# A two-layer hybrid attention decoder: the layer norm's statistics reordered on VectorE and TensorE, and spread by transposes

## The chip, the cores and the metric

The program runs on one core of one Trainium2 chip. The metric is the device time of one execution in microseconds; several executions are timed, and their median is given. One more execution is recorded by the hardware profiler, and all durations below come from that one.

## What is computed

Two decoder layers over 512 tokens of 1024 channels, in float32. Each layer has a mixing sub-layer and a feed-forward sub-layer, and each of them ends in a layer norm, so the program holds four layer norms in a row of dependent steps:

```python
u = x * (1.0 + sc1) + sh1
mix = token_mixer(u, w_in[l], ...)
x = layer_norm(ALPHA * x + (1.0 + g1) * mix, ln1_g[l], ln1_b[l])
u = x * (1.0 + sc2) + sh2
x = layer_norm(ALPHA * x + (1.0 + g2) * swiglu(u, w_ffn_in[l], w_ffn_out[l]), ln2_g[l], ln2_b[l])

def layer_norm(x, g, b):
    mu = jnp.mean(x32, -1, keepdims=True)
    var = jnp.mean(jnp.square(x32 - mu), -1, keepdims=True)
    return ((x32 - mu) * lax.rsqrt(var + EPS) * g + b).astype(x.dtype)
```

## The kernel before

Activations lie with channels on the 128 partitions: a tile of 1024 channels by 512 tokens is eight chunks (KD = 8) of 128x512. The residual stream is the tile `res`. A weight matrix is used in blocks of 128 output channels, called jobs: SyncE loads a block into one of two slots of `ring`, ScalarE rounds it into `w_hi` (L633), VectorE takes the rest into `w_lo` (L895, `prepare`; `prepare_behind` says with which chunk it is done), and TensorE multiplies three times for each pair of 128 channels: high by high (L1463), high by low input (L1464), low by high (L1465). The input of each sub-layer is split the same way into `u_hi` and `u_lo`. Every engine's instruction stream is written out by hand, in the order of the program text, and semaphores tie the streams together.

The layer norm after the mixing uses the chunks `wo0` to `wo7`, the one after the feed-forward the chunks `fo0` to `fo7`. For chunk m VectorE, in `layernorm`, does the split of a later weight block, subtracts a common shift from `res` (`unshift`, L1002; the shift is a channel sum that TensorE left in the bank `shift_ps`), adds the gated result of the sub-layer (L1017), adds the chunk to the running sum `t2` (L1035) and the squared chunk to the running sum of squares in `squares[:, 0]` (`add_square`, L1007). ScalarE makes the squares (L697). `link` makes the engine wait until the instruction it wraps has finished. The last chunk, m = 7, is not added to the running sums.

After the last chunk TensorE, in `mean_and_variance` (L1659 on), works in this order:

- `columns(mean_col, t2)`: four matmuls with one column each, which sum the seven chunks in `t2` over the partitions for 4x128 tokens (L1670); then the same for `res[:, 7]`, once L1017 has written it. This gives the mean, one token per partition, four columns.
- `columns(var_col, ...)`: the same for `squares[:, 0]` and `squares[:, 7]`.
- `keep_busy(2)`: two matmuls of 128x512 whose result nobody reads (L1685).
- `spread(mean_ps, 0)`: four matmuls of a broadcast column of `ln_s` with the identity, which put the mean of each token on all partitions (L1677). It waits for VectorE's copy of the mean (L1051).
- `keep_busy(4)`, then `spread(rstd_ps, 3)` for the reciprocal standard deviation, which waits for VectorE's reciprocal (L1057), then `keep_busy(9)` except in the last norm.

VectorE meanwhile does the weight split that the next sub-layer begins with, then `ada_part1` or `ada_part2` (`fold`, L978 to L983: five operations on 128x8 and a memset, which fold the norm's weights into the next input's scale and bias; only norms 0, 1 and 2 have it), then the four statistics operations: copy of the mean (L1051), its square (L1053), variance (L1055), and after ScalarE's square root (L702) the reciprocal (L1057). Then, chunk by chunk, it subtracts the spread mean (L1062) and multiplies by the spread reciprocal (L1065). ScalarE makes the new input from that (L644, L645), VectorE its low part (L1072), and TensorE's `project_first` starts on three weight blocks at once, chunk by chunk, as the chunks come. After the last norm TensorE turns `res` back to tokens on partitions (L1802) and the result is stored.

Numbering in this text: norm 0 and norm 1 are those of layer 0 (after mixing, after feed-forward), norm 2 and norm 3 those of layer 1.

Of the kernel before, what the change touches and what calls it, by code (L numbers as in the profile page):

```python
# [9 lines left out]
D_MODEL, SEQ, DEPTH = 1024, 512, 2  # L10
# [13 lines left out]
P = 128  # L24
# [173 lines left out]
def build(nc, x, w_ada, b_ada, c, w_in, pe_k, w1_k, w2_k, pe_v, w1_v, w2_v, lam, norm_g,  # L198
# [5 lines left out]
    with ctx:  # L204
# [50 lines left out]
        squares = at("squares", 46, KD)  # L255
# [56 lines left out]
        cos, sin, ident = cst[:, C_COS:C_COS + SEQ], cst[:, C_SIN:C_SIN + SEQ], cst[:, C_ID:C_ID + P]  # L312
# [3 lines left out]
        ln_s = sb("ln_s", [P, 4, TT])  # L316
# [23 lines left out]
        shift_ps, mean_col, var_col = banks[:, 2, :], banks[:, 3, 0:TT], banks[:, 4, 0:TT]  # L340
# [71 lines left out]
        sq_summed = sem("sq_summed")  # L412
# [27 lines left out]
        def wait_saved(eng, l, name):  # L440

            if name in THIRD:
                eng.wait_ge(third_saved, len(THIRD) * l + THIRD.index(name) + 1)
                return
            n = chunk(l, name)
            eng.wait_ge(chunk_saved[n % 2], n // 2 + 1)
# [431 lines left out]
        def _(dve):  # L878
# [3 lines left out]
            def link(ins):  # L882


                count[0] += 1
                ins.then_inc(dve_chain, 1)
                dve.wait_ge(dve_chain, count[0])
# [9 lines left out]
            def prepare_behind(l, name):  # L897
                for job in prepared_at(l, name):
                    prepare(*job)
# [6 lines left out]
            for k in FIRST_DVE:  # L906
# [3 lines left out]
                else:  # L910
                    ins = V.scalar_tensor_tensor(first_sum, ada_first[k], c_silu[:, k:k + 1], first_sum,
                                                 ALU.mult, ALU.add)
# [55 lines left out]
            def ada_part1(l):  # L968

                fold(l - 1, V_LN2G, V_LN2B, ada[:, l, 8:16], ada[:, l, 0:8], 0, 1, part1)  # L970

            def ada_part2(l):
                fold(l, V_LN1G, V_LN1B, ada[:, l, 32:40], ada[:, l, 24:32], 1, 0, part2)
# [22 lines left out]
            def layernorm(l, which):  # L996
                n = 2 * l + which
                names = [f"wo{m}" if which == 0 else f"fo{m}" for m in range(KD)]
                last_norm = l == DEPTH - 1 and which == 1
                def unshift(m):  # L1000

                    return V.scalar_tensor_tensor(res[:, m, :], shift_ps, -float(KD), res[:, m, :], ALU.mult, ALU.add)  # L1002

                def add_square(m):

                    dve.wait_ge(squared, n * KD + m + 1)
                    return V.tensor_tensor(squares[:, 0, :], squares[:, 0, :], squares[:, m, :], ALU.add)  # L1007

                for m in range(KD):
                    prepare_behind(l, names[m])  # L1010
                    if n >= 1 and m == 0:

                        dve.wait_ge(res_ready, n * KD)
                    if m >= 2:
                        link(unshift(m))
                    wait_done(dve, l, names[m])
                    V.scalar_tensor_tensor(res[:, m, :], bank_of(l, names[m]), gate1[:, l, which, m:m + 1],  # L1017
                                           res[:, m, :], ALU.mult, ALU.add).then_inc(saved(l, names[m]), 1)
                    if n == 0 and m == 4:
                        save_ada(2)  # L1020
                    elif n == 1 and m < 6:
                        add_ada_ffn(2 * KF + 2 * m)
                        add_ada_ffn(2 * KF + 2 * m + 1)
                        if m in (1, 4):
                            save_ada(7 + m // 4)
                    if m == 1:
                        dve.wait_ge(shift_done, n + 1)
                        wait_saved(dve, l, names[1])
                        for k in range(2):
                            unshift(k).then_inc(shifted, 1)  # L1030
                        dve.wait_ge(shifted, 2 * n + 2)
                        link(V.tensor_tensor(t2, res[:, 0, :], res[:, 1, :], ALU.add))
                    elif 2 <= m < KD - 1:
                        wait_saved(dve, l, names[m])
                        ins = V.tensor_tensor(t2, t2, res[:, m, :], ALU.add)  # L1035
                        if m == KD - 2:
                            ins.then_inc(y_summed, 1)
                        else:
                            link(ins)
                        link(add_square(m - 1))  # L1040
                        if m == KD - 2:
                            add_square(m).then_inc(sq_summed, 1)
                if not last_norm:
                    prepare(l + which, FIRST_SPLIT[which])
                if which == 0:
                    ada_part2(l)
                elif l + 1 < DEPTH:
                    ada_part1(l + 1)
                mean_s, var_s, rstd_s, square_s = (ln_s[:, k, :] for k in (0, 2, 3, 1))
                dve.wait_ge(mean_done, n + 1)  # L1050
                V.tensor_copy(mean_s, mean_col).then_inc(mean_saved, 1)  # L1051
                dve.wait_ge(mean_saved, n + 1)
                link(V.tensor_tensor(square_s, mean_s, mean_s, ALU.mult))  # L1053
                dve.wait_ge(var_done, n + 1)
                V.tensor_tensor(var_s, var_col, square_s, ALU.subtract).then_inc(var_ready, 1)  # L1055
                dve.wait_ge(std_ready, n + 1)
                V.reciprocal(rstd_s, var_s).then_inc(rstd_saved, 1)  # L1057
                for m in range(KD + 1):
                    if m < KD:
                        if m == 0:  # L1060
                            dve.wait_ge(mean_spread, n + 1)
                        link(V.tensor_tensor(res[:, m, :], res[:, m, :], mean_ps, ALU.subtract))  # L1062
                        if m == 0:
                            dve.wait_ge(rstd_spread, n + 1)
                        V.tensor_tensor(res[:, m, :], res[:, m, :], rstd_ps, ALU.mult).then_inc(normed, 1)  # L1065
                    if m and not last_norm:
                        sub_layer_low(n + 1, m - 1)
# [36 lines left out]
            for l in range(DEPTH):  # L1104
# [86 lines left out]
                for t in range(len(SEQUENCE) + 2):  # L1191
                    if 1 <= t <= len(SEQUENCE):
                        i, j = SEQUENCE[t - 1]
# [13 lines left out]
                    if t < len(SEQUENCE):  # L1207
                        i, j = SEQUENCE[t]
# [23 lines left out]
                    if 1 <= t <= len(SEQUENCE):  # L1232
                        i, j = SEQUENCE[t - 1]
# [8 lines left out]
                        if j <= 8:  # L1242
# [4 lines left out]
                            h, n = (0, 256) if j == 0 else (1, N)  # L1247
# [5 lines left out]
                    if t >= 2:  # L1253
                        i, j = SEQUENCE[t - 2]
# [126 lines left out]
        def _(pe):  # L1381
            M = nc.tensor.matmul
# [280 lines left out]
            def mean_and_variance(l, which):  # L1663

                n = 2 * l + which

                def columns(out, src, start, stop):

                    for i in range(TT):
                        ins = M(out[:, i:i + 1], src[:, i * P:(i + 1) * P], ones[:, 0:1], start=start and i == 0,  # L1670
                                stop=stop, skip_group_check=True)
                    return ins

                def spread(out, k):

                    for i in range(TT):
                        ins = M(out[:, i * P:(i + 1) * P], ln_s[:, k, i:i + 1].to_broadcast([P, P]), ident,  # L1677
                                start=True, stop=True)
                    return ins

                def keep_busy(count):

                    src = merged_hi if which == 0 else h_hi
                    for k in range(count):
                        M(shift_ps, src[:, 0, 0:P], src[:, 1, :], start=True, stop=True)  # L1685

                pe.wait_ge(y_summed, n + 1)
                columns(mean_col, t2, True, False)
                wait_saved(pe, l, ("wo", "fo")[which] + str(KD - 1))
                columns(mean_col, res[:, KD - 1, :], False, True).then_inc(mean_done, 1)  # L1690
                pe.wait_ge(sq_summed, n + 1)
                columns(var_col, squares[:, 0, :], True, False)
                pe.wait_ge(squared, (n + 1) * KD)
                columns(var_col, squares[:, KD - 1, :], False, True).then_inc(var_done, 1)
                keep_busy(2)
                pe.wait_ge(mean_saved, n + 1)
                spread(mean_ps, 0).then_inc(mean_spread, 1)
                keep_busy(4)
                pe.wait_ge(rstd_saved, n + 1)
                spread(rstd_ps, 3).then_inc(rstd_spread, 1)  # L1700
                if n + 1 < 2 * DEPTH:
                    keep_busy(9)

            for l in range(DEPTH):
                project_first(l, ("kc", "vc", "ksl")[:3 if l else 2], (u_hi, u_lo), u_ready, 2 * l * KD)
# [160 lines left out]
```

## Time and profile before

| | |
|---|---|
| median of 3 executions | 1799.22 us (1799.19 to 1803.18) |
| the profiled execution, its own time | 1796.96 us |
| its span, first to last instruction | 1795.1 us |
| TensorE matmul busy | 1700.7 us, 95% of the span |
| VectorE busy | 986.0 us, 55% |
| ScalarE busy | 633.2 us, 35% |
| TensorE's mean granted clock | 0.986 |
| chain that ended last | TensorE 83%, VectorE 7%, ScalarE 5%, issue 3%, DMA 2% |

The profiled execution took 1.9 us more than its span, which is what lies around the first and the last instruction. Granted clock 1.00 is TensorE's upper level of 2.4 GHz, 0.50 the lower of 1.2 GHz. A float32 matmul shows in the trace as two instructions (four `columns` matmuls are "x8"); a product of the rounded halves, a keep-busy matmul and a transpose show as one.

### The profile page before, as it was taken

Reading aid. Unit: us, or ns where it says so; the run is one execution under the profiler, and the core shown is the slowest. Engines: PE = TensorE matmul, PEld = TensorE weight load, DVE = VectorE, ACT = ScalarE, POOL = GpSimd, SP = SyncE. Lnnn points to the kernel's source line nnn. Section 1 sums busy time; section 2 is a strip of 40 time slices with the busy share of each in tenths; the row PEclk is TensorE's granted clock in tenths of the full one; section 3 lists DMA queues with packets and bytes.
Section 4 is the critical chain, followed back from the end, with each engine's and each line's share of the span. In section 5 each row is a group of like instructions: output and inputs, shape, how many; then the busy total and the mean of one; then the engine's idle time right before and its main releaser. Section 6 shows DMA issues by size and latency. Waiting matters only on the chain.

```text
span 1795.1 us, 21919 instructions
## 1 busy us (share of the span) xinstructions
PE 1700.7 (95%) x8620; PEld 1382.5 (77%) x8620; DVE 986.0 (55%) x1516; ACT 633.2 (35%) x1146; POOL 51.2 (3%) x100
## 2 busy tenths in 40 slices
PE   6899899899999999999989998899999999999997
PEld 5778667677787888888878776677777788888886
DVE  4776555656676555554557655555576633333344
ACT  0532344444334322222243324444452533222222
POOL 2000000000000000000000000000000000000000
PEclk9999999999999999999999999999999999999997
DMA  9554221113525666655426231100223233333331
GB/s 319 150 170 129 72 58 48 41 43 112 146 83 152 187 187 184 184 166 154 146 68 170 82 83 36 36 24 24 59 83 94 59 102 97 95 103 90 97 97 47
DMA packets 269686, 192.05 MB, mean 107 GB/s; under 512 B 8169, under 2 KB 254481, under 8 KB 268561
## 3 DMA queue, kind: packets, MB, share of 16 engines
q1 hardware_dynamic: 255632, 147.94, 28.2%
q0 software_dynamic: 12032, 42.07, 7.8%
q8 instruction: 69, 1.13, 0.3%
q10 hardware_dynamic: 1920, 0.66, 0.2%
q14 instruction: 33, 0.26, 0.0%
HBM read 188.54 MB, written 2.10 MB: 106 GB/s over the span
## 4 chain that ended last, share of the span: by engine, by line
PE 83%; DVE 7%; ACT 5%; issue 3%; DMA 2%; SPq 0%; ACTq 0%; DVEq 0%
PE banks L1463 22%; PE banks L1465 21%; PE banks L1464 21%; PE banks L1579 4%; PE banks L1613 3%; ACT probs L801 3%; PE banks L1638 3%; DVE w_lo L895 1%; DMA ring<-in_w_in_dram 1%; PE banks L1512 1%; PE banks L1514 1%; PE banks L1513 1%; PE banks L1581 1%; DMA ada_first_a<-in_w_ada_dram 1%; PE banks L1527 1%
## 5 line engine op out<-in xcount | busy, mean ns | idle before, releaser
L1463 PE MATMUL banks<-u_hi,w_hi 128*128 128x512 f32 x1216 | 499.2, 411 | 13.2 <-DVE w_lo L895 7.8
L1465 PE MATMUL banks<-u_hi,w_lo 128*128 128x512 f32 x1216 | 475.6, 391 | 0.0
L1464 PE MATMUL banks<-u_lo,w_hi 128*128 128x512 f32 x1216 | 475.4, 391 | 0.0
L895 DVE TENSOR_TENSOR w_lo<-ring,w_hi 128x1024 fp32r<-128x1024 f32 (+2 forms) x246 | 294.4, 1199 | 325.3 <-ACT w_hi L633 324.7
L633 ACT ACTIVATE w_hi<-ring 128x1024 fp32r<-128x1024 f32 (+2 forms) x246 | 253.7, 1032 | 230.3 <-PE banks L1465 102.2
L1463 PEld LDWEIGHTS banks<-u_hi,w_hi 128*128 128x128 f32 x1216 | 229.8, 189 | 55.2 <-DVE w_lo L895 9.5
L1465 PEld LDWEIGHTS banks<-u_hi,w_lo 128*128 128x128 f32 x1216 | 228.9, 188 | 49.5
L1464 PEld LDWEIGHTS banks<-u_lo,w_hi 128*128 128x128 f32 x1216 | 230.1, 189 | 36.9
L1463 PE MATMUL banks<-h_hi,w_hi 128*128 128x512 f32 x352 | 138.5, 394 | 0.0
L1465 PE MATMUL banks<-h_hi,w_lo 128*128 128x512 f32 x352 | 137.0, 389 | 0.0
L1464 PE MATMUL banks<-h_lo,w_hi 128*128 128x512 f32 x352 | 137.0, 389 | 0.0
L1230 DVE TENSOR_REDUCE neg_max<-banks 128x2 f32<-128x256 f32 (+3 forms) x96 | 79.1, 824 | 93.2 <-PE banks L1581 91.9
L781 ACT ACTIVATE probsT<-banks 128x128 f32<-128x128 f32 (+3 forms) x96 | 42.0, 437 | 214.7 <-PE banks L1613 214.7
L801 ACT ACTIVATE probs<-banks,neg_max 128x128 f32<-128x128 f32 (+3 forms) x192 | 99.0, 524 | 9.8 <-DVE neg_max L1230 9.8
L867 ACT ACTIVATE h_hi<-h_raw 128x512 fp32r<-128x512 f32 x44 | 27.8, 632 | 198.5 <-DVE h_raw L1358 198.5
L949 DVE SCALAR_TENSOR_TENSOR ada_acc<-ada_ring,c_silu,ada_acc 128x1024 f32<-128x1024 f32 x70 | 89.7, 1281 | 3.4 <-DMA ada_ring<-in_w_ada_dram 0.6
L1358 DVE TENSOR_TENSOR h_raw<-banks,raw 128x512 f32<-128x512 f32 x44 | 30.4, 691 | 108.5 <-PE banks L1465 108.5
L1638 PEld LDWEIGHTS banks<-v_tok,probsT 128*128 128x128 f32 x640 | 79.5, 191 | 3.8
L1638 PE MATMUL banks<-v_tok,probsT 128*128 128x64 f32 x640 | 78.3, 269 | 0.0
L1464 PEld LDWEIGHTS banks<-h_lo,w_hi 128*128 128x128 f32 x352 | 66.1, 188 | 13.8 <-issue 0.5
L1463 PEld LDWEIGHTS banks<-h_hi,w_hi 128*128 128x128 f32 x352 | 66.1, 188 | 13.7 <-issue 0.5
L1465 PEld LDWEIGHTS banks<-h_hi,w_lo 128*128 128x128 f32 x352 | 66.1, 188 | 13.8
(228 smaller groups left out, 2107.3 us busy)
## 6 DMA issues: line engine op xcount, KB each, us to landing
ring<-in_w_ffn_in_dram SPq DMA_DIRECT2D x88, 512.0 KB, 3.9
ada_ring<-in_w_ada_dram POOLq DMA_DIRECT2D x80, 512.0 KB, 4.3
ring<-in_w_in_dram SPq DMA_DIRECT2D x72, 512.0 KB, 3.8
ring<-in_w_ffn_out_dram SPq DMA_DIRECT2D x32, 448.0 KB, 3.6
ring<-in_w_out_dram SPq DMA_DIRECT2D x16, 512.0 KB, 3.9
ring<-in_w_ffn_out_dram SPq DMA_DIRECT2D x16, 512.0 KB, 4.1
ada_first_a<-in_w_ada_dram SPq DMA_DIRECT2D x5, 1024.0 KB, 9.5
w<-in_cmp_w_k_dram SPq DMA_DIRECT2D x8, 512.0 KB, 4.9
```

The source lines that it names most:

```text
L633: nc.scalar.activation(split_slot(l, name)[0], src, ACT.Copy).then_inc(split_hi, 1)
L781: nc.scalar.activation(probsT[:, s % 2, 0, 0:N], turned[:, 0, 0:N], ACT.Copy)\
L801: last = nc.scalar.activation(probs[:, s % 2, h, 0:N], scores[:, h, 0:N], ACT.Exp, bias=neg_max[:, s % 2, h:h + 1], accum_out=sums[:, i % ...
L895: V.tensor_tensor(lo, src, hi.bitcast(fp32), ALU.subtract).then_inc(split_lo, 1)
L949: V.scalar_tensor_tensor(acc, w, c_k, acc, ALU.mult, ALU.add).then_inc(ada_added, 1)
L1230: V.tensor_reduce(neg_max[:, s % 2, 0:2], scores[:, 0:2, 0:N], AX.X, ALU.max, negate=True).then_inc(max_done, 1)
L1463: M(bank, wh[:, block], sh[:, k, :], start=start, stop=False)
L1464: M(bank, wh[:, block], sl[:, k, :], start=False, stop=False)
L1465: return M(bank, wl[:, block], sh[:, k, :], start=False, stop=stop)
L1579: M(scores[:, h, 0:N], q, k, start=True, stop=True)
L1613: last = nc.tensor.transpose(turned[:, h, b * P:(b + 1) * P], src, ident)
L1638: last = M(bank[:, 64 * head:64 * head + 64], probsT[:, s % 2, h, b * P:(b + 1) * P], v_tok[:, b, v], start=b == 0, stop=b == i)
```

## The change

On VectorE `unshift(m)` goes ahead of the weight splits of its chunk, and `ada_part1`/`ada_part2` go behind the reciprocal. On TensorE the columns of `squares[:, 0]` go ahead of those of `res[:, 7]`; both spreads become transposes; `keep_busy(2)` and `keep_busy(4)` go, and `keep_busy(9)` becomes `keep_busy(8)`.

```diff
                 for m in range(KD):
+                    if m >= 2:
+                        link(unshift(m))
                     prepare_behind(l, names[m])
                     if n >= 1 and m == 0:
                         dve.wait_ge(res_ready, n * KD)
-                    if m >= 2:
-                        link(unshift(m))
                     wait_done(dve, l, names[m])
...
                 if not last_norm:
                     prepare(l + which, FIRST_SPLIT[which])
-                if which == 0:
-                    ada_part2(l)
-                elif l + 1 < DEPTH:
-                    ada_part1(l + 1)
                 mean_s, var_s, rstd_s, square_s = (ln_s[:, k, :] for k in (0, 2, 3, 1))
...
                 V.reciprocal(rstd_s, var_s).then_inc(rstd_saved, 1)
+                if which == 0:
+                    ada_part2(l)
+                elif l + 1 < DEPTH:
+                    ada_part1(l + 1)
                 for m in range(KD + 1):
...
                 def spread(out, k):
                     for i in range(TT):
-                        ins = M(out[:, i * P:(i + 1) * P], ln_s[:, k, i:i + 1].to_broadcast([P, P]), ident,
-                                start=True, stop=True)
+                        ins = nc.tensor.transpose(out[:, i * P:(i + 1) * P], ln_s[:, k, i:i + 1].to_broadcast([P, P]),
+                                                  ident)
...
                 pe.wait_ge(y_summed, n + 1)
                 columns(mean_col, t2, True, False)
+                pe.wait_ge(sq_summed, n + 1)
+                columns(var_col, squares[:, 0, :], True, False)
                 wait_saved(pe, l, ("wo", "fo")[which] + str(KD - 1))
                 columns(mean_col, res[:, KD - 1, :], False, True).then_inc(mean_done, 1)
-                pe.wait_ge(sq_summed, n + 1)
-                columns(var_col, squares[:, 0, :], True, False)
                 pe.wait_ge(squared, (n + 1) * KD)
                 columns(var_col, squares[:, KD - 1, :], False, True).then_inc(var_done, 1)
-                keep_busy(2)
                 pe.wait_ge(mean_saved, n + 1)
                 spread(mean_ps, 0).then_inc(mean_spread, 1)
-                keep_busy(4)
                 pe.wait_ge(rstd_saved, n + 1)
                 spread(rstd_ps, 3).then_inc(rstd_spread, 1)
                 if n + 1 < 2 * DEPTH:
-                    keep_busy(9)
+                    keep_busy(8)
```

TensorE at norm 0, the piece of the difference (the program's own instructions, a float32 matmul as one; `t` is `t2`, `cst` holds the identity):

```order
 L1670 MATMUL banks<-ones,t 128x1 x4
+L1670 MATMUL banks<-ones,squares 128x1 x4
 L1670 MATMUL banks<-ones,res 128x1 x4
-L1670 MATMUL banks<-ones,squares 128x1 x8
-L1685 MATMUL banks<-merged_hi 128x512 x2
-L1677 MATMUL banks<-cst,ln_s 128x128 x4
-L1685 MATMUL banks<-merged_hi 128x512 x4
-L1677 MATMUL banks<-cst,ln_s 128x128 x4
-L1685 MATMUL banks<-merged_hi 128x512 x9
+L1670 MATMUL banks<-ones,squares 128x1 x4
+L1677 MATMUL banks<-cst,ln_s 128x128 x8
+L1685 MATMUL banks<-merged_hi 128x512 x8
```

The columns of the running sum of squares moved ahead of `res`, six unread products between the groups are gone, and the two spreads stand next to each other.

VectorE at norm 0, before, from the last weight split to the first normalised chunk:

```order
483 L895 TENSOR_TENSOR w_lo<-ring,w_hi 128x1024
484 L978 TENSOR_TENSOR mul_u<-vec,ada 128x8
485 L979 TENSOR_TENSOR add_u<-vec,ada 128x8
486 L980 TENSOR_TENSOR add_u<-add_u,ada 128x8
487 L981 TENSOR_SCALAR mul_r<-vec 128x8
488 L982 TENSOR_SCALAR add_r<-vec 128x8
489 L983 MEMSET d_mix 128x1
490 L1051 COPY ln_s<-banks 128x4
491 L1053 TENSOR_TENSOR ln_s<-ln_s 128x4
492 L1055 TENSOR_TENSOR ln_s<-banks,ln_s 128x4
493 L1057 RECIPROCAL ln_s<-ln_s 128x4
494 L1062 TENSOR_TENSOR res<-res,banks 128x512
```

and the same stretch of the change (its statistics have the lines L1047 to L1053):

```order
483 L895 TENSOR_TENSOR w_lo<-ring,w_hi 128x1024
484 L1047 COPY ln_s<-banks 128x4
485 L1049 TENSOR_TENSOR ln_s<-ln_s 128x4
486 L1051 TENSOR_TENSOR ln_s<-banks,ln_s 128x4
487 L1053 RECIPROCAL ln_s<-ln_s 128x4
488 L978 TENSOR_TENSOR mul_u<-vec,ada 128x8
489 L979 TENSOR_TENSOR add_u<-vec,ada 128x8
490 L980 TENSOR_TENSOR add_u<-add_u,ada 128x8
491 L981 TENSOR_SCALAR mul_r<-vec 128x8
492 L982 TENSOR_SCALAR add_r<-vec 128x8
493 L983 MEMSET d_mix 128x1
494 L1062 TENSOR_TENSOR res<-res,banks 128x512
```

The six small operations of `fold` went from ahead of the mean's copy to between the reciprocal and the first normalised chunk. ScalarE's instructions are the same.

## Rows read from the trace of the kernel before

**Rows 1.** The page: busy time by engine, and the granted clock in 40 slices.

```profile
PE 1700.7 (95%) x8620; PEld 1382.5 (77%) x8620; DVE 986.0 (55%) x1516; ACT 633.2 (35%) x1146; POOL 51.2 (3%) x100
PEclk9999999999999999999999999999999999999997
```

**Rows 2.** Chain that ended last, norm 0: start us, us, what.

```profile
522.13 1.23 DVE w_lo L895
523.36 0.61 DVE res L1002
523.99 0.76 DVE res L1017
524.80 2.86 PE banks L1670 x24
527.66 1.06 PE banks L1685 x2
528.73 1.71 PE banks L1677 x8
530.43 1.20 PE banks L1685 x4
531.63 0.91 PE banks L1677 x8
532.63 0.70 DVE res L1065
...
535.70 0.47 PE banks L1463
```

**Rows 3.** Timeline, norm 0: start us, us, engine, line, operation [idle before, releaser].

```profile
523.08 0.40 PE L1465 MATMUL banks<-merged_hi,w_lo 128*128 128x512 f32 x1
...
523.31 0.95 PE L1670 MATMUL banks<-ones,t 128*128 128x1 f32 x8
...
525.87 0.16 DVE L978 TENSOR_TENSOR mul_u<-vec,ada 128x8 f32<-128x8 f32 x1
...
526.51 0.16 DVE L1051 COPY ln_s<-banks 128x4 f32<-128x4 f32 x1
...
527.77 0.16 DVE L1055 TENSOR_TENSOR ln_s<-banks,ln_s 128x4 f32<-128x4 f32 x1 [0.91 <-PE banks L1670]
...
528.29 0.18 DVE L1057 RECIPROCAL ln_s<-ln_s 128x4 f32<-128x4 f32 x1 [0.36 <-ACT ln_s L702]
```

**Rows 4.** Timeline, norm 1: from the first columns to the first normalised chunk.

```profile
909.21 0.95 PE L1670 MATMUL banks<-ones,t 128*128 128x1 f32 x8
...
909.48 0.75 DVE L1017 SCALAR_TENSOR_TENSOR res<-banks,gate,res 128x512 f32<-128x512 f32 x1 [2.47 <-PE banks L1465]
...
911.20 1.93 PE L1670 MATMUL banks<-ones,squares 128*128 128x1 f32 x16
...
918.10 0.69 DVE L1065 TENSOR_TENSOR res<-res,banks 128x512 f32<-128x512 f32 x1 [1.65 <-PE banks L1677]
```

**Rows 5.** Timeline, norms 2 and 3: first columns and first normalised chunk.

```profile
1393.96 0.95 PE L1670 MATMUL banks<-ones,t 128*128 128x1 f32 x8
...
1403.27 0.69 DVE L1065 TENSOR_TENSOR res<-res,banks 128x512 f32<-128x512 f32 x1 [1.25 <-PE banks L1677]
...
1768.40 0.95 PE L1670 MATMUL banks<-ones,t 128*128 128x1 f32 x8
...
1777.31 0.69 DVE L1065 TENSOR_TENSOR res<-res,banks 128x512 f32<-128x512 f32 x1 [2.50 <-PE banks L1677]
```

**Rows 6.** Transposes by line, attention and end of program: ns min/median/max, first and last start.

```profile
L1613 PEld LDWEIGHTS banks<-cst,probs x416: 137/140/144, 191.3 to 1274.2; 128*128 128x128 f32 x139
L1802 PEld LDWEIGHTS banks<-cst,res x32: 138/226/231, 1778.9 to 1789.9; 128*128 128x128 f32 x32
```

**Rows 7.** Stretches: us, busy PE, PEld, DVE, ACT, POOL, granted clock, DMA share, GB/s.

```profile
527.50:530.80 3.30, 3.30 (x14) 3.01 (x14) 0.67 (x3) 0.30 (x1) 0.00 (x0) 0.50 0.48 142
940.50:947.20 6.70, 5.12 (x15) 4.26 (x16) 6.25 (x14) 2.37 (x4) 0.00 (x0) 0.50 0.50 141
```

## The prediction

> **What bounds the kernel now.** First the page: TensorE is busy for 95% of the span, at the full clock nearly throughout [rows 1]. So time is to be had only where the products stop, and the change touches such a place, the layer norm, four times. Next the chain that ended last, at norm 0 [rows 2]: between the last product, which starts at 523.08 [rows 3], and the first product of the next sub-layer at 535.70, every step waits for the one before it. The reader should see that TensorE stands in that chain with 1.06 and 1.20 us of keep-busy matmuls, which nobody reads, and with 1.71 and 0.91 us for two spreads of the same size. The third view is the granted clock [rows 7]: it is 0.50 (1.2 GHz) from 527.5 to 530.8, behind four microseconds in which TensorE had only one-column matmuls, and that is why the first spread took 1.71 and the second, at 1.00 (2.4 GHz), 0.91. The timelines of the other norms show the same shape. From the first columns to the first normalised chunk (L1065) they take:
>
> - norm 0: 532.63 - 523.31 = 9.32 us [rows 2, 3]
> - norm 1: 918.10 - 909.21 = 8.89 us [rows 4]
> - norm 2: 1403.27 - 1393.96 = 9.31 us, norm 3: 1777.31 - 1768.40 = 8.91 us [rows 5]
>
> Behind L1065 nothing changes: at norm 0 the first product follows 535.70 - 532.63 = 3.07 us later [rows 2], and I take the program behind it as it was, only earlier.
>
> **The columns.** Eight instructions of one group take 0.95, and four groups in a row, as at norm 1, end at 911.20 + 1.93 = 913.13, 3.92 after they began, of which about 0.1 is a wait for L1017 [rows 4]. With the squares' running sum second, the group of `res` comes up 1.9 us after the first column, and L1017 is over long before that: at norm 0 it ends at 524.75 [rows 2], and TensorE gets there at 525.2. So four groups take 3.8 us without a gap in each norm. This also decides the price of the moved unshift. At norms 0 and 2 L1017 now waits for split and unshift (1.23, then 0.61 on the chain [rows 2]), starting 0.4 us later after its product than at norm 1, where it starts 0.1 after it (523.99 against 523.58; [rows 2 to 4]). That 0.4 is saved, but the moved columns would have hidden it anyway: I cost the moved unshift at nothing, 0.4 us at two norms if that cover were gone. The weight split behind the unshift was waiting for ScalarE's `w_hi` in any case; between 0.6 us later at worst and not later, I take not later, since its reader is two blocks behind.
>
> **From the last column to the reciprocal.** The reciprocal starts 528.29 - 527.66 = 0.63 after the columns' end and ends 0.81 after it [rows 2, 3]. Not touched.
>
> **The fold.** Its six operations take 526.51 - 525.87 = 0.64 us [rows 3]. Before, they stood ahead of the mean's copy, and VectorE then waited 0.91 us for the variance, so they were free. Now they stand between the reciprocal and L1062 in norms 0, 1 and 2. What is queued behind them is the normalising itself, for which everybody waits.
>
> **Spreads and keep-busy.** The spread of the mean no longer waits behind keep-busy matmuls: it starts at the end of the columns, and the copy of the mean, made in time (mean columns end at 2.85 after the first column), does not hold it. It is ready before VectorE is. A transpose in attention takes one weight load of 140 ns, at the half clock at the end of the program 226 [rows 6]; four take about 0.66 with the pipeline's end at full clock (estimate, 4 x 0.14 and 0.1 for the last one to land) and 1.1 at half. The spread of the reciprocal starts 0.06 after it and so is ready 3.8 + 0.81 + 0.06 + 0.66 to 1.1 = 5.3 to 5.8 us after the first column.
>
> **The sum.** In norms 0 to 2 VectorE reaches L1062 at 3.8 + 0.63 + 0.1 (the small operations overlap) + 0.64 = 5.17, and L1065 one such operation later (0.70 on the chain [rows 2]), at 5.87; the spread is there by then. Against 9.32, 8.89 and 9.31 that is 3.45 + 3.02 + 3.44 = 9.9 us. Norm 3 has no fold, and L1065 waits for the spread: 5.3 to 5.8 and a few hundredths; I take 5.7, so 3.2 us. Together 13.1 us.
>
> **What the clock takes back.** Nothing in the change keeps the clock up sooner: in all, TensorE now has 3.8 us of one-column matmuls and then 1.5 us of transposes and waiting before eight keep-busy matmuls. So I expect the drop to 0.50 again, at about the same place. At full clock the eight take 8 x 0.23 = 1.8 us (0.23 is the step from product to column, 523.08 to 523.31 [rows 3]) and end at about 7.8 us from the first column, before the first product could start at 5.87 + 3.07 = 8.94. At half clock they take twice that, 3.7 us, and end at 9.3: the products of three norms start 0.3 us later. I subtract 0.9 us. The sum is 12.2 us: 1796.96 - 12.2 = 1784.8 against the profiled execution's own time. The median of the runs shown is 2.3 us above that execution, so on the median's scale it is 1799.22 - 12.2 = **1787.0 us**, 0.68% faster.
>
> Bounds of what the trace doesn't show. The transpose of a broadcast column: at best the 140 ns of attention, at worst no cheaper than today's spread, 0.91 and 1.71. Behind the norms, the removed keep-busy matmuls: at best nothing, at worst a stretch at half clock under real products. The trace has one such stretch, 940.5 to 947.2, 6.7 us at 0.50 with TensorE busy for 5.1 of them [rows 7]; a stretch of T us costs T/2. At norm 0 the drop lasted 3.3 us [rows 7], and I am nearer to that row, for it is the same place.
>
> A rule of the skill speaks against this change. The Trainium skill, "TensorE: Matmul & The Clock Gate", section "Part 4: PE-mode transpose", says that the full clock does not engage for transposes, since they do not count as a busy array in the same way. In this trace attention has 416 such transposes of L1613 among matmuls at full clock, which neither shows nor refutes it, and at the end of the program transposes with pauses run at half. By that rule TensorE's light work would last 1.5 us longer, and the result would be that of rival A.
>
> **Rival A, the clock stays down under the products (0.12).** With keep-busy 2 and 4 gone and the 16 spread instructions now 8 transposes, the clock is still at 0.50 when `project_first` restarts. For it: TensorE's light work lasts longer than before, and what it did before already cost the clock at norm 0 [rows 7]. Against: eight keep-busy matmuls and then back-to-back products follow, and at norm 0 the drop was over after 3.3 us. One more stretch of 3.4 us of products at half in three norms costs 3 x 1.7 = 5.1 us: 1792.1. With stretches of 6.7 us it costs 10 us: 1797.
>
> **Rival B, slower (0.03).** The same gate, but it does not reopen for most of `project_first`. It decides from 2 x 12.2 / 3 = 8.1 us of products at half clock per norm. For it: the trace's 6.7 us stretch comes close. Against: that one had TensorE idle for 1.6 us, while `project_first` feeds it without a gap. With 12 us at half in three norms it loses 18 us: 1805.
>
> **Rival C, the transposes are not shorter (0.10).** They show as 8 instructions per spread like today's matmuls, at half clock 1.71 us each. Then the spread of the reciprocal is ready not before 3.8 + 1.71 + 1.71 + 0.1 = 7.3 us, and each norm gains 1.4 us less: 6 us of 12 are left with the keep-busy: 1793. Against: all transposes of float32 data in this trace are one instruction each [rows 6].
>
> **How the numbers follow.** The forecast has 0.75: VectorE's path through the fold sets L1065, and it hardly depends on the transposes. Its own bounds are 1783 (no delay from the clock, and the executions' own scatter of 2 us downwards) and 1790. The range reaches on to rival A's first price and rival C: 1783 to 1793. About 0.3% (5.4 us) is what a measurement of this kernel can tell from no change, so faster means below 1793.8: the forecast, most of A and C, 0.88. Within 0.3%: A with long stretches and part of C, 0.09. Slower: rival B, 0.03.
>
> **What would show it.** Right: L1065 of the first chunk 5.7 to 6.0 us after the first columns in every norm; 32 column instructions without a gap; spreads of 4 instructions; VectorE's L978 to L983 right behind the reciprocal, with L1062 behind them and not behind TensorE; the first product 3.1 us after L1065; a granted clock that falls behind the columns and is back at 1.00 by the first product, or shortly after. Wrong: a granted clock of 0.50 in the first microseconds of `project_first`, spreads of 8 instructions, or a wait of L1062 for TensorE. If the first products start on time and the total still moves by less than 9 us, the loss is behind the norms, in the clock or in the blocks whose loads I took as following along.

## The result and the profile after

The changed kernel takes 1786.89 us in the median of five executions (1783.10 to 1790.99); the kernel before, in five beside them, 1801.80 (1799.19 to 1803.18). The ratio is 0.992, with a 95% interval from 0.990 to 0.9939. That is 14.9 us faster; the forecast was 12.2 us faster, 1787.0 us on the scale of the three executions shown then. A second set of six gave 1786.50 against 1801.86, ratio 0.9926 (0.9913 to 0.9939).

The page of the changed kernel, its line of busy time, answers to [rows 1]:

```profile
PE 1693.6 (95%) x8561; PEld 1375.3 (77%) x8561; DVE 987.6 (55%) x1516; ACT 633.4 (35%) x1146; POOL 51.3 (3%) x100
```

TensorE has 59 instructions fewer, VectorE and ScalarE as many as before; so what was saved is time in a chain, not work of an engine that is the bound. The chain that ended last, at norm 0 of the changed kernel (start us, us, what), answers to [rows 2]:

```profile
527.38 3.48 PE banks L1670 x32
530.86 0.03 issue
...
530.96 0.17 DVE ln_s L1051
...
531.15 0.31 ACT ln_s L702
...
531.48 0.19 DVE ln_s L1053
...
531.72 1.13 PE banks L1677 x4
...
532.94 0.70 DVE res L1065
...
536.01 0.47 PE banks L1463
```

All 32 column instructions now stand in it as one piece, and no keep-busy matmul (L1685) does. Of the two spreads only that of the reciprocal is left, with four instructions. The timeline of the same place has the rest (columns as in [rows 3]):

```profile
526.99 0.40 PE L1465 MATMUL banks<-merged_hi,w_lo 128*128 128x512 f32 x1
527.22 0.95 PE L1670 MATMUL banks<-ones,t 128*128 128x1 f32 x8
...
530.71 2.12 PE L1677 MATMUL banks<-cst,ln_s 128*128 128x128 f32 x8
...
531.58 0.14 DVE L978 TENSOR_TENSOR mul_u<-vec,ada 128x8 f32<-128x8 f32 x1
...
532.19 0.68 DVE L1062 TENSOR_TENSOR res<-res,banks 128x512 f32<-128x512 f32 x1
...
532.48 2.94 PE L1685 MATMUL banks<-merged_hi 128*128 128x512 f32 x8
532.94 0.69 DVE L1065 TENSOR_TENSOR res<-res,banks 128x512 f32<-128x512 f32 x1
```

From the first columns to L1065 norm 0 takes 532.94 - 527.22 = 5.72 us, where it took 9.32. The clock, in stretches of the changed kernel as in [rows 7] (granted clock third from the end):

```profile
530.90:534.30 3.40, 3.31 (x12) 2.57 (x11) 2.80 (x12) 0.93 (x2) 0.00 (x0) 0.50 0.53 154
534.40:551.00 16.60, 16.01 (x71) 12.96 (x70) 13.26 (x21) 12.23 (x18) 0.00 (x0) 1.00 0.00 1
```

It falls behind the columns as before, for 3.4 us, and is back 1.7 us ahead of the first product at 536.01. Under the products it is full. The same holds at norms 1 and 2. Norm 3, which has no keep-busy matmuls behind it in either kernel, is different: the clock fell at 1766.5 and stayed at 0.50 to the end of the program, where only transposes with pauses follow:

```profile
1766.60:1785.00 18.40, 9.48 (x35) 5.88 (x33) 13.46 (x22) 7.59 (x10) 0.00 (x0) 0.50 0.31 115
```

The kernel before had it at 0.50 from 1773.4 to 1776.8 and again from 1780.2 on. This cost nothing that can be seen: of the 3.41 us that norm 3 gained, 3.36 arrive at the end of the span. Over the program:

| from first columns to | before | after | saved |
|---|---|---|---|
| L1065, norm 0 | 9.32 us | 5.72 us | 3.60 |
| L1065, norm 1 | 8.89 | 5.72 | 3.17 |
| L1065, norm 2 | 9.31 | 5.72 | 3.59 |
| L1065, norm 3 | 8.91 | 5.50 | 3.41 |
| norm 0 to norm 1, first columns to first columns | 385.90 | 382.34 | 3.56 |
| norm 1 to norm 2 | 484.75 | 481.38 | 3.37 |
| norm 2 to norm 3 | 374.44 | 370.82 | 3.62 |
| norm 3 to the end of the span | 26.70 | 23.34 | 3.36 |

What a norm gains at L1065 arrives at the next norm to within 0.2 us: 13.8 us at the four L1065, 13.9 us over these stretches. The two profiled spans differ by only 10.0 us (1795.1 and 1785.1), since the changed kernel's profiled execution reached norm 0 3.9 us later (527.22 against 523.31). The change does not touch what lies ahead of the wo chunks, and thirteen profiled executions of all the kernels of this study reach norm 0 anywhere from 523.3 to 527.2 us. This is why the parts below are compared by norm as well as by median.

### The profile page after: what moved, and what is told of

It is laid out like the page before. It is cut to its first block, busy times and chain, and to the rows that moved or that the text cites. A ratio compares the mean times of both kernels' runs of the same rounds, so it can differ in the third digit from the quotient of the medians.

```text
span 1785.1 us, 21777 instructions
## 1 busy us (share of the span) xinstructions
PE 1693.6 (95%) x8561; PEld 1375.3 (77%) x8561; DVE 987.6 (55%) x1516; ACT 633.4 (35%) x1146; POOL 51.3 (3%) x100
## 4 chain that ended last, share of the span: by engine, by line
PE 84%; DVE 6%; ACT 4%; issue 3%; DMA 2%; SPq 0%; ACTq 0%; DVEq 0%
PE banks L1463 23%; PE banks L1465 22%; PE banks L1464 22%; PE banks L1579 4%; PE banks L1613 3%; PE banks L1638 3%; ACT probs L801 3%; DVE w_lo L895 1%; PE banks L1512 1%; PE banks L1513 1%; PE banks L1514 1%; DMA ring<-in_w_in_dram 1%; PE banks L1581 1%; DMA ada_first_a<-in_w_ada_dram 1%; PE banks L1527 1%
```

## The experiments

Each ran on one core; each median is beside executions of the kernel before on the same chip. "L1065" means the time from the first columns to the first L1065 (or what that line is called there) of norms 0, 1, 2, 3 in the profiled execution. The kernel before has 9.32, 8.89, 9.31, 8.91, the changed one 5.72, 5.72, 5.72, 5.50.

### The parts alone, on the kernel before

**Only the unread products.**

```diff
-                keep_busy(2)
...
-                keep_busy(4)
...
-                    keep_busy(9)
+                    keep_busy(8)
```

> The kernel before with only the unread products changed (2 and 4 gone, 9 to 8); matmul spreads, old column order, fold ahead. Theory (the keep-busy matmuls stand in the serial chain): both spreads now run back to back behind the columns, both at the half clock, 1.71 us each, so the first normalised chunk (L1065) comes 7.4 to 7.9 us after the first column in place of 8.9 to 9.3. That is 1.45 us a norm, 5.8 us in all. Rival (they only fill time in which TensorE would wait for the statistics): no change, 8.9 to 9.3 us stay. A second rival (transposes carry the change): less than 2 us.

Measured: 1793.25 against 1800.76 us, ratio 0.9958 (0.9945 to 0.9971), so 7.5 us. L1065: 7.95, 6.50, 7.95, 8.31. Its chain at norm 0:

```profile
526.68 2.87 PE banks L1670 x24
529.55 3.51 PE banks L1677 x16
...
533.15 0.70 DVE res L1065
```

Both spreads, 16 instructions, now run back to back for 3.51 us at the half clock, as the theory had it. At norm 1 the clock fell later and the 16 took 2.61, so 2.4 us were gained there. The theory's 5.8 us lies within the measured interval (5.2 to 9.9 us), and the four L1065 give 5.7. The rival of no change falls, and so does the one that leaves this edit less than 2 us: it is half of the whole.

**Only the transposes.**

```diff
-                        ins = M(out[:, i * P:(i + 1) * P], ln_s[:, k, i:i + 1].to_broadcast([P, P]), ident,
-                                start=True, stop=True)
+                        ins = nc.tensor.transpose(out[:, i * P:(i + 1) * P], ln_s[:, k, i:i + 1].to_broadcast([P, P]),
+                                                  ident)
```

> The kernel before with only the spreads as transposes. Theory: the first spread shrinks from 1.71 to about 0.9 us at half clock, the second from 0.91 to 0.66 at full clock; the keep-busy matmuls between them stay in the chain. 1.0 us a norm, 4 us in all, L1065 8.0 to 8.3 us after the first column. Rival (the transposes show as eight instructions per spread, like matmuls): nothing. Rival of the clock (transposes do not count as work, so the low clock lasts longer): the granted clock stays at 0.50 for longer than 3.5 us behind the columns in some norm, and the gain is under 2 us.

Measured: 1799.44 against 1800.76 us, ratio 0.9991 (0.9982 to 1.000). L1065: 8.40, 7.28, 8.39, 9.39, so 0.92, 1.61, 0.92 gained and 0.48 lost. This is a miss: 1.3 us (interval 0 to 3.2), where 4 were expected; the four L1065 give 3.0. Its chain at norm 0 shows why:

```profile
531.32 1.71 PE banks L1685 x4
533.03 0.56 PE banks L1677 x4
...
533.68 0.70 DVE res L1065
```

The spread did shrink to four instructions. But the low clock lasted 3.4 us all the same, so the four keep-busy matmuls behind the shortened spread now ran fully inside it: 1.71 us, where they took 1.20 in [rows 2]. Part of what the transposes save, the keep-busy matmuls hand back. The transposes' worth depends on the removal beside them. The gap between the 3.0 us of the norms and the 1.3 us of the medians has a place in the profile too: the granted clock is 0.50 for 3.4 us at 1065.6 and again at 1096.3, in the attention of layer 1, where the kernel before has 1.00, and TensorE falls back by 2.7 us there. Whether all twelve executions have these two stretches is not known.

The rival of the clock asked for a low stretch of more than 3.5 us in some norm and a gain under 2 us. Both came: at norm 3 the clock was down for 6.8 us. But the two kernels of the next experiments, whose spreads are still matmuls, have the same 6.8 us at norm 3, so the transposes are not needed for it. At norms 0 to 2 it is 3.4 us in each, as before.

**Only the column order.**

```diff
                 columns(mean_col, t2, True, False)
+                pe.wait_ge(sq_summed, n + 1)
+                columns(var_col, squares[:, 0, :], True, False)
                 wait_saved(pe, l, ("wo", "fo")[which] + str(KD - 1))
                 columns(mean_col, res[:, KD - 1, :], False, True).then_inc(mean_done, 1)
-                pe.wait_ge(sq_summed, n + 1)
-                columns(var_col, squares[:, 0, :], True, False)
```

> The kernel before with only the column order changed (running sum of squares ahead of res). Theory: the four column groups run without a gap, 3.63 us, and end 0.7, 0.3, 0.9 and 0.3 us earlier than before in norms 0 to 3; 2.2 us in all, L1065 that much earlier. Rival (VectorE's later statistics, not the columns, set the spread): nothing.

Measured: 1798.73 against 1800.76 us, ratio 0.9988 (0.9977 to 0.9999), which is 2.0 us (interval 0.2 to 4.1), where 2.2 were expected. The columns take 3.63 to 3.65 us at norms 0 to 2 in place of 4.35, 3.92 and 4.57. L1065: 8.62, 8.61, 8.61, 10.23. The gain of norms 0 to 2 (0.70, 0.28, 0.70) is what the columns gained or less, so the rival falls. Norm 3 lost 1.3 us: the clock was at 0.50 for 6.8 us there, from 1771.0, in the middle of the columns, to 1777.8; in the profile of the kernel before it fell behind them and for half as long. The profile thus shows 1.7 us at norms 0 to 2, where 1.9 were expected, and no gain at norm 3.

**Only the unshift.**

```diff
+                    if m >= 2:
+                        link(unshift(m))
                     prepare_behind(l, names[m])
...
-                    if m >= 2:
-                        link(unshift(m))
```

> The kernel before with only the unshift moved ahead of the splits. Theory: in norms 0 and 2 L1017 of the last chunk starts 0.4 us earlier, the columns end 0.4 us earlier, L1065 comes 0.4 us earlier in two norms, norms 1 and 3 stay: 0.8 us in all, within 0.3% of the kernel before. Rival (the split is made later by the unshift and TensorE waits for weights): new waits of TensorE for w_lo in the wo chunks, slower.

Measured: 1798.23 against 1800.73 us, ratio 0.9987 (0.9977 to 0.9996). L1065: 8.82, 8.82, 8.82, 10.45. Alone it gives 0.50 us at norm 0, 0.07 at norm 1, 0.49 at norm 2, about as expected; norm 3 lost 1.5 us, with the clock down for 6.8 us there as in the run before. The median's 2.5 us is more than these make, and its interval reaches down to 0.7. No wait of TensorE for `w_lo` appeared at the end of the wo chunks.

### One part undone, on the changed kernel

**The unshift back behind the splits.**

```diff
-                    if m >= 2:
-                        link(unshift(m))
                     prepare_behind(l, names[m])
...
+                    if m >= 2:
+                        link(unshift(m))
                     wait_done(dve, l, names[m])
```

> The changed kernel with only the unshift back behind the splits. Theory: L1017 of the last chunk starts 0.4 us later in norms 0 and 2, but the columns of the running sum of squares cover it: columns still 3.6 us, L1065 still at 5.7 us, same time as the changed kernel. Rival (the unshift is in the chain): columns 4.0 us in norms 0 and 2.

Measured: 1785.16 us (four executions), ratio to before 0.9912 (0.990 to 0.9925). The columns take 3.62 and 3.63 us, L1065: 5.71, 5.73, 5.72, 5.26. The time is 1.3 to 1.7 us below the changed kernel's two medians, which is within the scatter of the executions. So beside the new column order the moved unshift is worth nothing, as expected. Its 0.5 us and the column order's 0.7 are the same wait, removed twice.

**The fold back ahead of the mean's copy.**

```diff
                     prepare(l + which, FIRST_SPLIT[which])
+                if which == 0:
+                    ada_part2(l)
+                elif l + 1 < DEPTH:
+                    ada_part1(l + 1)
                 mean_s, var_s, rstd_s, square_s = (ln_s[:, k, :] for k in (0, 2, 3, 1))
...
                 V.reciprocal(rstd_s, var_s).then_inc(rstd_saved, 1)
-                if which == 0:
-                    ada_part2(l)
-                elif l + 1 < DEPTH:
-                    ada_part1(l + 1)
```

> The changed kernel with the fold back ahead of the mean's copy. Theory: L1062 starts 0.64 us earlier, but L1065 then waits for the transposes of the reciprocal, which at half clock are ready only 0.1 us before L1065 starts now. So 0.05 us a norm where the clock has dropped, up to 0.5 where it has not: 0.2 to 1 us in all, too little for the median, and L1065 waits for TensorE (L1677) in norms 0 to 2. Rival (the fold is fully in the chain): 0.64 us in each of three norms, 1.9 us.

Measured: 1786.57 us, ratio to before 0.9918 (0.9905 to 0.9932). L1065: 5.73, 5.72, 5.73, 5.30. The timeline at norm 0:

```profile
529.68 0.66 DVE L1062 TENSOR_TENSOR res<-res,banks 128x512 f32<-128x512 f32 x1
...
529.82 1.12 PE L1677 MATMUL banks<-cst,ln_s 128*128 128x128 f32 x4 [0.38 <-DVE ln_s L1057]
...
531.05 0.69 DVE L1065 TENSOR_TENSOR res<-res,banks 128x512 f32<-128x512 f32 x1 [0.71 <-PE banks L1677]
```

L1062 comes 0.6 us earlier and L1065 then waits 0.71 us for the transposes, which take 1.12 at the half clock. The fold and the transposes last equally long beside each other: moving the fold neither costs nor gains while the clock is down there. The rival, 0.64 us a norm, falls.

**Matmuls in place of the transposes.** The diff of "only the transposes", reversed, on the changed kernel.

> The changed kernel with the spreads as matmuls again. Theory: both spreads run back to back from 3.6 us after the first column, at half clock at least the second, so the spread of the reciprocal lands at 6.5 (first one at full clock) to 7.3 us in place of 5.6, and L1065 waits for TensorE: 0.8 to 1.6 us a norm, 3 to 6.5 us slower than the changed kernel, 1790 to 1793. Rival (the transposes are nothing, VectorE's path through the fold sets L1065): same as the changed kernel, L1065 at 5.7 us.

Measured: 1791.13 us, ratio 0.9946 (0.9933 to 0.9959), 4.2 to 4.6 us more than the changed kernel's two medians. Those were not taken beside it, but the traces agree: from norm 0's first columns to the end of the span it takes 1262.1 us, the changed kernel 1257.9. L1065: 7.26, 5.76, 6.68, 6.61, and it waits for TensorE:

```profile
528.67 3.47 PE L1677 MATMUL banks<-cst,ln_s 128*128 128x128 f32 x16
...
530.76 0.69 DVE L1062 TENSOR_TENSOR res<-res,banks 128x512 f32<-128x512 f32 x1 [0.53 <-PE banks L1677]
...
532.24 0.69 DVE L1065 TENSOR_TENSOR res<-res,banks 128x512 f32<-128x512 f32 x1 [0.80 <-PE banks L1677]
```

So the transposes, worth 1 to 3 us alone, are worth over 4 once the keep-busy matmuls are gone. Norm 1 shows from the other side what the low clock costs: there it did not fall, the 16 instructions took 2.16 us, and L1065 came at 5.76, against 5.72 with transposes. So at the full clock the shorter spread is worth 0.04 us, because VectorE's fold takes as long; what it is worth, it is worth in the low stretch.

**No unread products at the end of the norm.**

```diff
-                    keep_busy(8)
+                    keep_busy(0)
```

> The changed kernel without the last eight unread products of each norm. Theory (they are what brings the clock back before the new input comes): behind the columns TensorE now does nothing from 5.6 to 8.8 us after the first column, so the granted clock is 0.50 for about 7 us or more in norms 0 to 2 in place of 3.5, and the first 2 to 5 us of the products run at half: 1 to 2.5 us a norm, 3 to 7.5 us slower than the changed kernel, 1790 to 1794. L1065 stays at 5.7 us. Rival (with back-to-back products behind them they aren't needed, the first products themselves bring it back at once): under 1 us.

Measured: 1795.26 us (1794.95 to 1796.00), ratio 0.9968 (0.9956 to 0.998): 8.4 to 8.8 us slower than the changed kernel, more than the theory's 7.5. From norm 0's first columns to the end of the span the profile is 10.1 us longer than the changed kernel's. L1065 is unchanged at 5.72, 5.69, 5.71 (norm 3, which never had the tail, 6.34, since the clock fell in the middle of its columns). At norm 0 the stretch and the products in it:

```profile
534.30:539.90 5.60, 5.60 (x13) 4.40 (x14) 5.50 (x10) 3.93 (x6) 0.00 (x0) 0.50 0.01 3
```

```profile
534.27 0.76 PE L1463 MATMUL banks<-u_hi,w_hi 128*128 128x512 f32 x1 [3.18 <-DVE u_lo L1072]
534.84 0.63 PE L1464 MATMUL banks<-u_lo,w_hi 128*128 128x512 f32 x1
535.26 0.63 PE L1465 MATMUL banks<-u_hi,w_lo 128*128 128x512 f32 x1
...
540.17 0.39 PE L1465 MATMUL banks<-u_hi,w_lo 128*128 128x512 f32 x1
```

The clock is 0.50 from 529.7 to 539.9, and thirteen products are issued 0.43 us apart in place of 0.23. Norm 2 has the same (10.2 us):

```profile
1400.10:1410.40 10.30, 6.90 (x18) 5.28 (x19) 9.80 (x22) 6.40 (x9) 0.00 (x0) 0.51 0.15 44
```

At norm 1 it is 6.8 us. This is rival A of the prediction, made to happen by taking away the tail that the change kept. Under the products behind norms 0, 1 and 2 TensorE falls back by 2.6, 1.4 and 2.7 us, 6.7 us in all. The rest lies elsewhere: 2.7 us in two stretches of 3.4 us at 0.50, at 1065.6 and 1096.3, in the attention of layer 1, and 0.8 us at norm 3. The profile of "only the transposes" has the same two stretches, with its tail in place, and the other eleven profiles have neither; so whether the missing tail brings them is not shown.

**Twelve in place of eight.**

```diff
-                    keep_busy(8)
+                    keep_busy(12)
```

> The changed kernel with twelve unread products at the end of each norm in place of eight. Theory (the eight end at 8.2 to 8.5 us after the first column where the clock has dropped, the new input comes at 8.8): twelve run into the new input, 0.3 to 1.2 us a norm, 1 to 3.5 us slower than the changed kernel; the clock is no better. Rival (a longer tail saves the clock in executions in which eight are too few): faster than the changed kernel by 1 us or more.

Measured: 1787.78 us (1786.11 to 1789.76), ratio 0.993 (0.9917 to 0.9942), beside 1786.50 for the changed kernel. The first product comes 9.24, 9.04 and 8.97 us after the first columns in norms 0 to 2, where it came at 8.79: 0.9 us of new waiting. The medians differ by 1.3 us, within what they scatter; the rival of a faster kernel did not come, and the 0.9 us lies just under the expected 1 to 3.5. The norms show that eight end just in time (8.1 to 8.5 us) and twelve do not (9.1 to 9.4).

**The changed kernel again.**

> The changed kernel once more, beside the next two on the same chip. Theory: 1785 to 1789 us; L1065 5.7 us after the first column in norms 0 to 2, the clock down for one stretch of about 3.5 us behind the columns of norms 0 to 2 and back before the new input.

Measured: 1786.50 us (1784.47 to 1789.35). L1065: 5.72, 5.72, 5.72, 5.29, first products at 8.79 in all three norms, one stretch of 3.4 us at 0.50 behind the columns of each of norms 0 to 2.

### A wait elsewhere filled

```diff
+                if l:
+                    for k in range(16):
+                        M(shift_ps, u_hi[:, 0, 0:P], u_hi[:, 1, :], start=True, stop=True)
                 project(l, "kwn")
```

> The changed kernel with sixteen unread products (128x512 from the new input) in the wait of 4.3 us that TensorE has in layer 1 between its first three blocks and the fourth (before kwn). Nothing of the result is changed. Theory (as with the tail: what TensorE does in a wait decides the clock of the products behind it): the drop of 6.9 us at about 936 to 944 us goes away, and with it up to half of the 5.1 us of products in it, 1 to 2.5 us faster than the changed kernel. Rival (VectorE and ScalarE set the pace there, not TensorE): the drop goes and the time stays.

Measured: 1786.15 us (1784.22 to 1787.98), beside 1786.50. The clock first, for this kernel and then for the changed one at the same place:

```profile
935.00:943.00 8.00, 7.30 (x37) 5.85 (x36) 5.00 (x12) 4.33 (x7) 0.00 (x0) 1.00 0.32 85
```

```profile
935.10:942.00 6.90, 4.95 (x15) 4.08 (x15) 6.08 (x14) 2.75 (x4) 0.00 (x0) 0.51 0.46 136
```

The drop is gone, as intended. The time is not: from norm 1's first columns to norm 2's it takes 481.07 us against 481.37. The timeline shows what took the drop's place:

```profile
939.13 0.50 PE L1463 MATMUL banks<-u_hi,w_hi 128*128 128x512 f32 x1 [0.70 <-DVE w_lo L895]
...
951.95 0.40 PE L1512 MATMUL banks<-w_hi,u_hi 128*128 128x280 f32 x1 [0.52 <-DVE w_lo L895]
957.65 0.40 PE L1512 MATMUL banks<-w_hi,u_hi 128*128 128x280 f32 x1 [0.75 <-DVE w_lo L895]
```

TensorE, at full clock, waits for the next weight splits. Counted from norm 1's first columns, its products are 2.2 us ahead of the changed kernel's at 950 us and 0.4 us ahead at 1000. The rival was right: the low clock cost at most the 0.3 us that is left at norm 2.

## Why the prediction was right

**The place and the path.** As forecast: the serial chain of four norms, and nothing given back behind it. Norms 0 to 2 reach L1065 at 5.72 us (forecast 5.87), norm 3 at 5.50 and 5.29 (forecast 5.7). The products follow at 8.79 (forecast 8.94).

**The columns.** Forecast 3.8 us, measured 3.63. The 0.15 us at L1065 is this term; the others were hit to 0.05 us. Four groups of eight issue closer than [rows 4] suggested with the wait taken out.

**The unshift at nothing, under the columns' cover.** Shown: 0.5 us at norms 0 and 2 alone, nothing beside the column order.

**The fold.** Here the working was wrong in part, without harm. It put 0.64 us of the fold into the chain and had the spread of the reciprocal ready by then. It was ready hardly sooner. The transposes end 532.85 - 527.22 = 5.63 us after the first column, L1065 starts at 5.72, and without the fold it starts at 5.73. The step "VectorE's path sets L1065, and it hardly depends on the transposes" should have read: fold and transposes at the half clock are a tie. The forecast had both numbers (5.87, and 5.3 to 5.8) and did not draw the conclusion. At the full clock the step holds, as norm 1 of the run without the tail shows, where the clock fell only 4.9 us after the first columns:

```profile
914.94 0.75 PE L1677 MATMUL banks<-cst,ln_s 128*128 128x128 f32 x4 [0.38 <-DVE ln_s L1053]
...
915.41 0.68 DVE L1062 TENSOR_TENSOR res<-res,banks 128x512 f32<-128x512 f32 x1
...
916.13 0.69 DVE L1065 TENSOR_TENSOR res<-res,banks 128x512 f32<-128x512 f32 x1
```

The transposes end at 915.69, 0.4 us ahead of L1065, which waits for nothing and still comes at 5.69 us: the path through the fold alone.

**What the clock takes back.** Forecast 0.9 us, measured nothing. The clock fell where it was expected, but it came back before the eight keep-busy matmuls were over, so they took 2.9 us and not 3.7, and ended at 8.1 to 8.5 us, ahead of the input. The term was mis-sized by counting all eight at half clock, although its own row for the length of the drop, 3.3 us [rows 7], spoke against it, and by a start that was too late: they begin at 5.27, so that even at half clock throughout they would have ended at about 9.0 (estimate, 5.27 + 3.7), 0.2 us behind the first product's 8.79. The two ends in the working do not fit each other either: 7.8 at full clock means a start at 6.0, 9.3 at half one at 5.6. And 9.3 - 8.94 in three norms is 1.1 us, not 0.9.

**The sum.** With columns and clock put right, 12.2 becomes 13.8 us, which is what the four L1065 show. That 1787.0 was hit to 0.1 us is luck: the median of before on which it stood, 1799.22, was 1801.8 with two more executions. A gain too small by 2.7 us by the medians (1.7 by the traces) and a base too low by 2.6 us met.

**The rule behind rival A.** The Trainium skill, "TensorE: Matmul & The Clock Gate", section "Part 4: PE-mode transpose", says that transposes do not engage the full clock. From it the prediction drew rival A, which did not come: in both profiles of the changed kernel the clock came back 3.4 us after it fell in each of norms 0 to 2. Transposes and keep-busy matmuls stood in that time together, so the rule itself is neither shown nor refuted. Norm 3 does not decide it either. Transposes alone follow there and the clock stayed at 0.50 for the last 18 us, but TensorE was idle for half of that time, and the kernel with matmul spreads has the same from norm 3 to its end. Only the price that the rule threatened is measured, when the tail goes: 6.7 us behind three norms.

**The rivals.** A did not come, and the run without the tail shows that it was near: its chance of 0.12 rested on eight matmuls. The price of a low stretch, half its length, holds: 5.6 us of products at 0.50 cost 2.6 us at norm 0. B (slower) is further off than was thought: even with no tail the drop lasted 10.2 us, of which 5.6 under products, and the kernel was still faster than before. C (transposes no shorter) is out: four instructions a spread, and 4.2 to 4.6 us lost when they are matmuls again.

## What to carry to other kernels

Filler work on a serial chain is paid for; the same filler behind the last step that anybody waits for is free and can be worth much. Here the six unread products ahead of and between the spreads took 2.26 us of the chain at norm 0 [rows 2], of which their removal alone gave back 1.37, since the second spread then ran at half clock. Over four norms their removal, together with that of the ninth product behind the spreads, was worth 7.5 us. The eight behind the spreads save at least 6.7. Price the parts of a change together: two edits that remove the same wait count once (unshift and column order), and two that stand in the same low-clock stretch are worth more together than one of them alone (transposes and the removed products). Before a low clock is repaired, look at what the products under it wait for next.

## What was not expected of the hardware

- The changed norms 0 to 2 give the same times to 0.01 us in nearly all profiles (5.71 to 5.73 us, 8.79 us), while the unchanged first part of the program ends anywhere in a range of 3.9 us. The profiles differ there in where the granted clock is low: about 36 to 50 us in the kernel before, 36 to 53 in the changed one, with two more stretches of 3.4 us near 193 and 224. The thirteen profiles sort by these: two with neither stretch reach norm 0 at 523.3 and 523.9 us, nine with one at 525.0 to 525.9, two with both at 527.1 and 527.2.
- Norm 3 took 8.91 us in the profiled execution of the kernel before, but 9.39, 10.23 and 10.45 in three kernels that are the same there but for one part. In those the clock was low for 6.8 us, in place of 3.4, and it fell 2.3 to 2.8 us after the first columns, in place of 4.95. The changed kernel's norm 3 took 5.50 and 5.29, but there the clock fell at 4.8 and 5.0 us; without the tail it fell at 2.8, and norm 3 took 6.34. So where the drop begins matters in both kernels. Whether this makes up the last microsecond between the 13.9 us of the profiles and the 14.9 us of the medians stays open.
- Taking away 1.8 us of unread matmuls (at full clock) lengthened the low stretch from 3.4 to 10.2 us at two norms.
